# A third seven-product pair in the second feed forward, with one pair's weight sums kept in DRAM

## Chip, cores and metric

One core of one Trainium2 chip. The metric is the device time of one execution in microseconds (us): median of three runs, lower is better.

## What is computed

Two transformer blocks on x of 256 rows by 1024 columns, in fp32. The part that the change touches is the gated feed forward of the second block, and, as a place for early work, the feed forward of the first:

```python
def sq_relu_mlp(h, w1, w2):                       # first block, D_FF = 4096
    return jnp.square(jax.nn.relu(h @ w1)) @ w2

# second block, D_FF_2 = 2816
h = rmsnorm(x, norm_ffn[layer])
x = x + (jax.nn.silu(h @ w_gate[layer]) * (h @ w_up[layer])) @ w_down[layer]
return rmsnorm(x, norm_final)
```

## The kernel before

Each engine has its own program, written out by hand in the order in which it runs: `tensor_program` (TensorE, PE), `vector_program` (VectorE, DVE), `scalar_program` (ScalarE, ACT), `pool_program` (GpSimd, POOL) and `sync_program`, whose queue (SP) issues the weight loads. They meet at semaphores alone.

**Three products for one.** A weight tile of 1 MB (128 partitions x 2048) is a `Unit`. It lands in one of six slots (seven in the second feed forward), ScalarE makes its high half (`hi`, line 1185), VectorE the low half (`lo`, line 1720), two instructions of 128x1024 each. `part` (lines 511 to 513) then multiplies, for each k of the unit, high by high, high by low and low by high: four k make 12 matmuls of 128x512. I call that a product.

**The second feed forward.** The 2816 columns are eleven chunks of 256. `GROUPS` lists them as single chunks and as pairs of chunks; `PAIRS = (3,7)` makes two pairs, so that the groups are chunks 0, 1, 2, (3,4), 5, 6, (7,8), 9, 10. A single chunk takes two gate-and-up units for each of the two row blocks, 4 products, so two single chunks take 8. A pair takes 7 for the same columns, on a Winograd form of the 2x2 block product: three of the units are used as loaded, four are sums. The weight sums are made in place by VectorE (`make`, two instructions of 128x1024 for each of four sums), the input sums once (`form`). Against its 7 products a pair has 7 gate-and-up units and 2 down units to load and split, where two single chunks have 4 and 2.

**The order in a group.** `begin(g)` is the group's first product or two, `rest(g)` what follows, with the down products of group g-1 inside. After a pair, TensorE runs `begin(g + 1)` and only then turns the pair's hidden rows (`hid_turn2`, eight transposes, line 493); ScalarE and VectorE make high and low halves of the turned rows (`hid_lo2`, line 2055, semaphore `hid_lo`), and the down products of the pair, `down2(g, ...)`, wait for these. In `quad_group` VectorE makes the pair's hidden rows between splits of weight units. After the loop over groups the end is written out: the last chunk's gate-and-up product (`up2`), the down products of the last two groups, and the last turns.

**The first feed forward** (about 180 to 350 us) has `up_wide` and `down1` on TensorE; VectorE runs `sum_wide`, `low_wide`, splits, and rows of an adaptive gate (`gate_rows`). Tiles S1 and S2 (16 KB of each partition) lie idle during most of it, until `between` writes S1 again at its end.

Of the kernel before, what the change touches and what calls it, by code (L numbers as in the profile page):

```python
# [24 lines left out]
class Mem:  # L25


    def __init__(self, nc, ctx):
# [116 lines left out]
        self.FL = [M(f"FL{i}", 68 + 2 * i, [128, 4, 128], F32R) for i in range(4)]  # L145
        self.g1 = M("quad_g1", 6, [128, 512])
# [19 lines left out]
out_mm o1_hi o1_lo res1 nscale_dve nscale_act n_turned n_dve n_act kn  # L166
# [7 lines left out]
out2_mm res2 made quad_act quad gu_mm dn_mm hid2 res3 last_rows y_out y_act""".split()  # L174
# [16 lines left out]
class Unit:  # L191
# [3 lines left out]
    def __init__(self, nk, wid, pieces, split, free):  # L195
        self.nk, self.wid, self.pieces, self.split, self.free = nk, wid, pieces, split, free
        self.base = None
# [13 lines left out]
PAIRS = (3,7)  # L211
# [15 lines left out]
def weight_units(d, S):  # L227
# [68 lines left out]
    def quad_unit(g, n, src, i):  # L296
        c0 = 256 * GROUPS[g][0]
        add(("gu", g), src, 4 * i, 4, [(src, c0, 512)], True, ("gu_mm", QUAD_AT[g] + n + 1))
        return units[-1]

    loads = list(units)
    for g in range(NG + 1):
        if g < NG and GROUPS[g][1]:
            quad_unit(g, 0, "w_gate_2", 0)
            quad_unit(g, 1, "w_up_2", 0)
            at = len(units)
            down_units(g - 1)
            down = units[at:]
            quad_unit(g, 2, "w_up_2", 1)
# [4 lines left out]
            b11, t1, t2, b22, t3, b21, t4 = by["gu", g]  # L314
            loads += [b11, t1, t2, *down, t4, b22, t3, b21]
# [16 lines left out]
    for g in range(NG):  # L332
        if GROUPS[g][1]:
            q = by["gu", g]
            used += [*q[0:3], *by["dn", g - 1], *q[3:7]]
        else:
            used += by["gu", g] + (by["dn", g - 1] if g else [])
# [22 lines left out]
    for n, g in enumerate(g for g in range(NG) if GROUPS[g][1]):  # L360
# [3 lines left out]
        t1.landed, t2.landed, t4.landed, t3.landed = ((S["made"], 8 * n + 2 * i + 2) for i in range(4))  # L364
# [3 lines left out]
def sync_program(e, m, S, units, by, out, d):  # L368
# [11 lines left out]
    def load(n):  # L380
        unit = units[n]
        for old in unit.old:
            w.wait_ge(old.free[0], old.free[1])
        v = unit.block(m)
# [21 lines left out]
def pool_program(e, m, S, d):  # L406
# [20 lines left out]

    e.dma_start(m.vec[:, :], d["vec"]).then_inc(S["l_vec"], 16)
# [22 lines left out]
    w.wait_ge(S["res1"], 8)  # L451
    e.dma_start(m.g1b[:, :], d["final_g"].to_broadcast([128, D])).then_inc(S["l_gain"], 16)
    power(6)
# [5 lines left out]
    for i in range(10, 14):  # L459
        power(i)  # L460


def tensor_program(e, m, S, by):
# [331 lines left out]
    def out1(i, tb):  # L795
# [3 lines left out]
        if k0:  # L799
            frees(2 * n + tb, ("res1", 4 * tb + 2 * n + 1))  # L800
# [253 lines left out]
    def out2(j, tb):  # L1054
# [3 lines left out]
        if i:  # L1058
            frees(2 * n + tb, ("res2", 2 * tb + n + 1))
# [29 lines left out]
    def down2(g, tb, first, last, ns=(0, 1)):  # L1089
        for n in ns:  # L1090
            for i, unit in enumerate(by["dn", g]):
                part(unit, m.HH[g % 2], m.HL[g % 2], 2 * i, tb, 2 * n + tb, first and i == 0, last, "dn_mm",
# [7 lines left out]
    def begin(g):  # L1100
        if GROUPS[g][1]:
            part(by["gu", g][0], m.AH, m.AL, 0, 0, 4, True, True, "gu_mm", n_ready(2, 0))
            quad_sum(g, 1, 0, 5, True)
# [36 lines left out]
    for g in range(2, NG - 1):  # L1140
        rest(g)
        if GROUPS[g][1]:
# [8 lines left out]
    up2(NG - 1, 0)  # L1151
# [18 lines left out]
def scalar_program(e, m, S, units, by, out, d):  # L1170
# [232 lines left out]
    s = norm_squares(4, "res1", (2, 4), 0)  # L1403
# [7 lines left out]
    s = norm_squares(6, "res1", (6, 8), 1)  # L1411
# [194 lines left out]
    s = norm_squares(16, "res2", (1, 2), 0)  # L1606
# [7 lines left out]
    s = norm_squares(18, "res2", (3, 4), 1)  # L1614
# [22 lines left out]
    def quad_group(g):  # L1637
# [14 lines left out]
        hi(2)  # L1652
# [5 lines left out]
    hi()  # L1658
    silu_gate(0, 1)
# [7 lines left out]
    for i in range(4):  # L1667
        form_hi(i)
    for g in range(2, NG - 1):
# [8 lines left out]
        for tb in range(2):  # L1678
            hid_hi2(g, tb)
# [4 lines left out]
    def last_squares(tb):  # L1684
        w.wait_ge(S["kn"], 12)
        for n, (c0, cw) in enumerate(LAST[tb]):
            w.wait_ge(S["res3"], 3 * tb + n + 1)
# [15 lines left out]
def vector_program(e, m, S, units, by):  # L1703
# [354 lines left out]
    def residual1(n, tb):  # L2058
# [6 lines left out]
        tt(m.S1[:, tb, hn], bank[2 * n + tb][:, :], m.g1b[:, hn], ALU.mult, "res1")  # L2065
        w.wait_ge(S["res1"], i + 1)
        tt(m.X[:, tb, hn], m.X[:, tb, hn], m.S1[:, tb, hn], ALU.add, "res1")
# [9 lines left out]
    def norm_features(call, tb, A, B):  # L2077
# [15 lines left out]
        tt(m.AL[:, 0:4, ts], hv, m.AH[:, 0:4, ts].bitcast(F32), ALU.subtract, "kn")  # L2093
        w.wait_ge(S["n_act"], 5 * call + 5)
# [61 lines left out]

    hid_lo(0, 4, 0, 1)
    lo(2)
    hid_lo(0, 4, 1, 2)
    lo(2)  # L2160
    for tb in range(2):
        hid_lo(1, 4, tb, 3 + tb)
    lo()
    for c in range(2, 7):
# [11 lines left out]
        else:  # L2176
            gate_add()
    sum_wide(7, 0)
# [42 lines left out]

    between(0, 2)
# [438 lines left out]
```

## Time and profile before

| | |
|---|---|
| three runs | 721.14 us median (720.99 to 721.19) |
| profiled execution | 720.66 us, its span 718.9 us |
| busy share of the span | PE 99%, PE weight loads 79%, DVE 77%, ACT 59%, POOL 4% |
| DMA | 152.22 MB, mean 212 GB/s |

The span is from the first to the last record; the 1.8 us around it are the execution's start and end. A busy share says only that an engine had an instruction under way: matmuls overlap, so that each of 0.39 us starts 0.23 us after the one before. The rows that the prediction rests on stand in a section of their own.

### The profile page before, as it was taken

The numbers are of one execution on the slowest core, as the hardware profiler recorded it, in microseconds if no ns is written. First come the engines' busy times: TensorE is split into PE (matmuls) and PEld (weight loads), VectorE is DVE, ScalarE is ACT, GpSimd is POOL, SyncE is SP. The second block draws the span as 40 slices with busy tenths as digits, with TensorE's granted clock in tenths as the row PEclk, the third lists the DMA queues.
The fourth block names the chain that finished last, engine by engine and source line by source line (L and its number), as shares of the span: only waits on it lengthen the run. The fifth ranks groups of instructions, "written<-read, shape, count | busy, mean of one in ns | idle before, by whom it ended". The sixth has DMA issues, their size and how long they took to land.

```text
span 718.9 us, 9667 instructions
## 1 busy us (share of the span) xinstructions
PE 709.1 (99%) x3722; PEld 567.9 (79%) x3722; DVE 555.8 (77%) x949; ACT 424.6 (59%) x701; POOL 25.9 (4%) x43
## 2 busy tenths in 40 slices
PE   8999999999999999999999999999999999999996
PEld 4678885588888888888888777778888888888885
DVE  4789999898666757756998799855857988678933
ACT  4487658995754654546645677666456466436712
POOL 1030012001000000000010000000000000000000
PEclk9999999999999999999999999999999999999999
DMA  9996939617556585744548433344375598568501
GB/s 366 415 378 224 387 104 357 218 59 263 197 179 231 214 289 196 268 146 154 163 144 300 172 118 118 119 172 178 118 233 175 197 313 310 181 230 316 209 1 58
DMA packets 71932, 152.22 MB, mean 212 GB/s; under 512 B 4096, under 2 KB 19456, under 8 KB 70864
## 3 DMA queue, kind: packets, MB, share of 16 engines
q1 hardware_dynamic: 70080, 146.32, 57.4%
q0 software_dynamic: 1520, 5.03, 2.0%
q8 instruction: 29, 0.48, 0.3%
q10 hardware_dynamic: 288, 0.27, 0.1%
q14 instruction: 15, 0.12, 0.0%
HBM read 150.56 MB, written 1.05 MB: 211 GB/s over the span
## 4 chain that ended last, share of the span: by engine, by line
PE 91%; ACT 3%; issue 2%; DMA 2%; DVE 1%; POOL 0%; POOLq 0%; DVEq 0%; SPq 0%
PE bank L511 23%; PE bank L513 23%; PE bank L512 23%; PE bank L856 5%; PE bank L493 5%; PE bank L854 3%; DMA W<-in_w_in 2%; ACT WH L1185 1%; PE bank L530 1%; PE bank L988 1%; PE bank L1010 1%; PE bank L694 1%; PE bank L716 1%; PE bank L570 1%; PE bank L853 1%
## 5 line engine op out<-in xcount | busy, mean ns | idle before, releaser
L1720 DVE TENSOR_TENSOR WL<-W,WH 128x1024 fp32r<-128x1024 f32 (+2 forms) x234 | 263.4, 1173 | 27.0 <-ACT WH L1185 26.7
L1185 ACT ACTIVATE WH<-W 128x1024 fp32r<-128x1024 f32 (+2 forms) x234 | 222.9, 1013 | 55.7 <-DMA W<-in_w_mlp 35.8
L511 PE MATMUL bank<-WH,AHL 128*128 128x512 f32 (+1 forms) x440 | 173.1, 393 | 0.0
L513 PE MATMUL bank<-WH,AHL 128*128 128x512 f32 (+1 forms) x440 | 169.7, 386 | 0.0
L512 PE MATMUL bank<-WL,AHL 128*128 128x512 f32 (+1 forms) x440 | 169.6, 385 | 0.0
L511 PEld LDWEIGHTS bank<-WH,AHL 128*128 128x128 f32 x440 | 82.7, 188 | 19.0 <-issue 3.2
L513 PEld LDWEIGHTS bank<-WH,AHL 128*128 128x128 f32 x440 | 82.6, 188 | 16.9
L512 PEld LDWEIGHTS bank<-WL,AHL 128*128 128x128 f32 x440 | 82.8, 188 | 15.4
L511 PE MATMUL bank<-WH,HH 128*128 128x512 f32 (+1 forms) x218 | 84.9, 390 | 0.0
L513 PE MATMUL bank<-WH,HL 128*128 128x512 f32 (+1 forms) x218 | 84.5, 388 | 0.0
L512 PE MATMUL bank<-WL,HH 128*128 128x512 f32 (+1 forms) x218 | 84.4, 387 | 0.0
L856 PE MATMUL bank<-AHL,WH 128*128 128x512 f32 x168 | 60.5, 398 | 0.0
L854 PE MATMUL bank<-AHL,WL 128*128 128x256 f32 x192 | 50.0, 281 | 0.0
L513 PEld LDWEIGHTS bank<-WH,HL 128*128 128x128 f32 x218 | 40.9, 188 | 8.5
L512 PEld LDWEIGHTS bank<-WL,HH 128*128 128x128 f32 x218 | 41.0, 188 | 8.3
L511 PEld LDWEIGHTS bank<-WH,HH 128*128 128x128 f32 x218 | 40.9, 188 | 8.0
L854 PEld LDWEIGHTS bank<-AHL,WL 128*128 128x128 f32 x192 | 36.3, 189 | 2.0
L856 PEld LDWEIGHTS bank<-AHL,WH 128*128 128x128 f32 x168 | 31.6, 188 | 6.7
L1735 DVE SCALAR_TENSOR_TENSOR cacc<-hp,vec,cacc 128x256 f32<-128x256 f32 x88 | 36.0, 479 | 0.2
L413 POOL TENSOR_TENSOR stat<-stat 128x1 f32<-128x1 f32 x12 | 10.1, 846 | 594.4 <-DVE stat L1744 549.0
L1193 ACT ACTIVATE HH<-bank 128x256 fp32r<-128x256 f32 (+1 forms) x22 | 9.2, 458 | 35.7 <-PE bank L493 35.7
L2055 DVE TENSOR_TENSOR HL<-bank,HH 128x256 fp32r<-128x256 f32 (+1 forms) x22 | 10.7, 517 | 23.4 <-ACT HH L1193 23.4
(307 smaller groups left out, 937.8 us busy)
## 6 DMA issues: line engine op xcount, KB each, us to landing
W<-in_w_mlp SPq DMA_DIRECT2D x32, 1024.0 KB, 5.4
W<-in_w_in SPq DMA_DIRECT2D x24, 1024.0 KB, 5.1
W<-in_w_down SPq DMA_DIRECT2D x11, 1024.0 KB, 5.1
W<-in_w_ada SPq DMA_DIRECT2D x10, 1024.0 KB, 8.0
WX<-in_w_ada SPq DMA_DIRECT2D x10, 1024.0 KB, 10.0
W<-in_w_out SPq DMA_DIRECT2D x8, 1024.0 KB, 5.2
W<-in_w_up SPq DMA_DIRECT2D x8, 1024.0 KB, 5.1
W<-in_w_gate SPq DMA_DIRECT2D x14, 512.0 KB, 4.0
```

The source lines that it names most:

```text
L413: e.tensor_tensor(m.stat[:, 40 + i:41 + i], m.stat[:, 24 + i:25 + i], m.stat[:, 94:95], ALU.pow).then_inc(S["rstd"], 1)
L493: ins = e.transpose(bank[b][:, c * 128:c * 128 + 128], src, m.ident[:, :])
L511: e.matmul(po, hs, wh[:, k, c0:c0 + cw], start=first and k == 0, stop=False, skip_group_check=onto)
L512: e.matmul(po, hs, wl[:, k, c0:c0 + cw], start=False, stop=False, skip_group_check=onto)
L513: ins = e.matmul(po, ls, wh[:, k, c0:c0 + cw], start=False, stop=last and k == unit.nk - 1, skip_group_check=onto)
L854: ins = e.matmul(bank[4 + j][:, 0:256], wl[:, k, js], m.AH[:, 4 * i + k, :], start=False, stop=False)
L856: ins = e.matmul(both, wh[:, k, js], m.AHL[:, :, 4 * i + k, :], start=False, stop=i == 1 and k == 3)
L1185: e.activation(m.WH[unit.slot][:, c], m.W32[unit.slot][:, c], ACT.Copy).then_inc(S["w_hi"], 1)
L1193: e.activation(o, i, ACT.Copy, scale=scale).then_inc(S[sem], 1)
L1720: e.tensor_tensor(m.WL[unit.slot][:, c], m.W32[unit.slot][:, c], m.WH[unit.slot][:, c].bitcast(F32), ALU.subtract).then_inc(S["w_lo"], 1)
L1735: e.scalar_tensor_tensor(o, a, scalar, b, op0, op1).then_inc(S[sem], 1)
L2055: e.tensor_tensor(L[:, k0:k0 + nj, ts], bank[b][:, 0:nj * 128].rearrange("p (j n) -> p j n", j=nj), H[:, k0:k0 + nj, ts].bitcast(F32), ALU ...
```

## The change

- `PAIRS` becomes (2, 5, 8): groups are chunks 0, 1, (2,3), 4, (5,6), 7, (8,9), 10. There are three pairs, and the last pair now stands directly ahead of the last chunk.
- The four weight sums of the pair at chunk 2 are made in the first feed forward and kept in a DRAM tensor `sums`: POOL loads the four blocks of 128x512 that belong to one k (two loads of 512 KB), VectorE makes four sums of 128x512 in place (`kept_sums`), and POOL stores the 1 MB. There are four such steps, in two staging places (offsets 0 and 8 KB, where S1 and S2 are). The second feed forward loads these sums as units; the pairs at 5 and 8 make theirs in place as before.
- `form` and `form_hi` move ahead, since a pair now comes as the third group. After the last pair `begin` already runs the last chunk's first `up2`, so the one after the loop is left out.

```diff
-PAIRS = (3,7)
+PAIRS = (2, 5, 8)
+STORED = (2,)
+STEPS = (4, 0, 0)
+SUMS_AT = (1, 0, 1, 0, 0, 0, 2, 0, 0, 0, 0, 0, 0)
+SUMS = [[(0, 8)[s % 2] for s in range(STEPS[0])], [0] * STEPS[1], [(68, 76)[s % 2] for s in range(STEPS[2])]]
...
     def quad_unit(g, n, src, i):
...
+        if GROUPS[g][0] in STORED and n in (1, 2, 4, 6):
+            s = STORED.index(GROUPS[g][0])
+            kept = d["sums"][s, {4: 0, 2: 1, 1: 2, 6: 3}[n]].rearrange("p (k n) -> p k n", k=4)
+            units[-1].pieces = [(0, 512, kept)]
...
+    def blocks_in(phase, i):
...
+        if SUM_AT[s]:
+            w.wait_ge(landing, SUM_AT[s])
+        if i < 2 and phase == 0:
+            w.wait_ge(*((S["n_turned"], 4), (S["kn"], 4))[i])
...
+        for j, src in enumerate(("w_up_2", "w_gate_2")):
+            rows = d[src][:, c0:c0 + 512].rearrange("(h k p) n -> p k h n", h=2, p=128)[:, kt, :, :]
+            e.dma_start(place[:, 2 * j:2 * j + 2, :], rows).then_inc(landing, 16)
...
     e.dma_start(m.g1b[:, :], d["final_g"].to_broadcast([128, D])).then_inc(S["l_gain"], 16)
+    kept_sums(0)
     power(6)
...
-    up2(NG - 1, 0)
+    if not GROUPS[NG - 2][1]:
+        up2(NG - 1, 0)
     down2(NG - 2, 0, False, False, (0,))
     hid_turn2(NG - 1, 0)
     down2(NG - 2, 0, False, False, (1,))
...
+    def kept_sums(place):
+
+        for s in range(sum(SUMS_AT[:place]), sum(SUMS_AT[:place + 1])):
+            at = m.sums[sum(SUMS, [])[s]]
+            u0, u1, g0, g1 = (at[:, i, :] for i in range(4))
+            w.wait_ge(S[f"l_sums{SUM_SEM[s]}"], SUM_AT[s] + 32)
+            tt(g0, u0, g0, ALU.subtract, "made")
+            tt(u0, u1, u0, ALU.subtract, "made")
+            w.wait_ge(S["made"], 4 * s + 1)
+            tt(u1, u1, g0, ALU.subtract, "made")
+            w.wait_ge(S["made"], 4 * s + 3)
+            tt(g1, g1, u1, ALU.subtract, "made")
...
     for tb in range(2):
         hid_lo(1, 4, tb, 3 + tb)
     lo()
+    kept_sums(1)
     for c in range(2, 7):
...
             gate_add()
+        kept_sums(c)
...
+    sums_stored()
     between(0, 2)
...
-        following = GROUPS[g + 1][1]
-        make(g, 2)
+        made, following, near = in_place(g), in_place(g + 1), GROUPS[g + 1][1]
+        if made:
+            make(g, 2)
```

TensorE, after the turns of the last pair's hidden rows (HH and HL are the high and low halves of turned hidden rows, AHL the input's, WH and WL a weight unit's). Before:

```order
L511 MATMUL bank<-WH_66,AHL 128x512
L512 MATMUL bank<-WL_60,AHL 128x512
L513 MATMUL bank<-WH_66,AHL 128x512
L493 MATMUL bank<-ident,hid_164 128x128 [waits hid2]
L493 MATMUL bank<-ident,hid_164 128x128 x3
L493 MATMUL bank<-ident,hid_164 128x128 [waits quad,hid2]
L493 MATMUL bank<-ident,hid_164 128x128 x3
L511 MATMUL bank<-WH_65,AHL 128x512
L512 MATMUL bank<-WL_59,AHL 128x512
L513 MATMUL bank<-WH_65,AHL 128x512
```

and now:

```order
L572 MATMUL bank<-WH_64,AHL 128x512
L552 MATMUL bank<-ident,hid_164 128x128 [waits hid2]
L552 MATMUL bank<-ident,hid_164 128x128 x3
L552 MATMUL bank<-ident,hid_164 128x128 [waits quad,hid2]
L552 MATMUL bank<-ident,hid_164 128x128 x3
L570 MATMUL bank<-WH_66,HH_166 128x512 [waits w_lo,hid_lo]
L571 MATMUL bank<-WL_60,HH_166 128x512
L572 MATMUL bank<-WH_66,HL_168 128x512
```

Before, 24 matmuls on AHL (two products of the next chunk) follow the turns, and then the down products on HH; now a down product, which waits for `hid_lo`, follows at once. Twelve down matmuls later come the two turns of the last chunk's hidden rows, which wait for `hid2`.

VectorE, at the same place. Before (the group behind the last pair was chunk 9):

```order
L1729 TENSOR_TENSOR quad_g_224<-bank,quad_g_224 128x512 [waits gu_mm]
L1720 TENSOR_TENSOR WL_60<-W_5_54,WH_66 128x1024 [waits w_hi] x2
L1729 TENSOR_TENSOR hid_164<-g1b,rel_170 128x512 [waits quad,silu,hid_turned]
L1729 TENSOR_TENSOR hid_164<-g1b,rel_171 128x512 [waits silu]
L1720 TENSOR_TENSOR WL_57<-W_2_51,WH_63 128x1024 [waits w_hi] x2
L1720 TENSOR_TENSOR WL_55<-W_0_49,WH_61 128x1024 [waits w_hi] x2
L2055 TENSOR_TENSOR HL_168<-bank,HH_166 128x4x128 [waits hid_hi] x2
L1720 TENSOR_TENSOR WL_210<-W_6_209,WH_211 128x1024 [waits w_hi] x2
L1729 TENSOR_TENSOR hid_165<-bank,rel_170 128x256 [waits hid_turned,silu]
```

and now:

```order
L1802 TENSOR_TENSOR quad_g_228<-bank,quad_g_228 128x512 [waits gu_mm]
L1793 TENSOR_TENSOR WL_58<-W_3_52,WH_64 128x1024 [waits w_hi] x2
L1802 TENSOR_TENSOR hid_164<-g1b,rel_170 128x512 [waits quad,silu,hid_turned]
L1802 TENSOR_TENSOR hid_164<-g1b,rel_171 128x512 [waits silu]
L1793 TENSOR_TENSOR WL_60<-W_5_54,WH_66 128x1024 [waits w_hi] x2
L1793 TENSOR_TENSOR WL_57<-W_2_51,WH_63 128x1024 [waits w_hi] x2
L2128 TENSOR_TENSOR HL_168<-bank,HH_166 128x4x128 [waits hid_hi] x2
L1793 TENSOR_TENSOR WL_55<-W_0_49,WH_61 128x1024 [waits w_hi] x2
L1802 TENSOR_TENSOR hid_165<-bank,rel_170 128x256 [waits hid_turned,silu]
L2128 TENSOR_TENSOR HL_169<-bank,HH_167 128x2x128 [waits hid_hi]
```

Operation for operation the first nine rows are the same, in other slots: nothing moved on VectorE here, while TensorE's next step did.

POOL, in the first feed forward, now:

```order
L507 DMA g1b<-in_final_g 128x1024 [waits res]
L466 DMA sums_224<-in_w_up 128x2x512 [waits n_turned]
L466 DMA sums_224<-in_w_gate 128x2x512
L466 DMA sums_225<-in_w_up 128x2x512 [waits kn]
L466 DMA sums_225<-in_w_gate 128x2x512
L477 DMA sums<-sums_224 128x4x512 [waits made]
L466 DMA sums_224<-in_w_up 128x2x512 [waits l_sums0]
L466 DMA sums_224<-in_w_gate 128x2x512
L477 DMA sums<-sums_225 128x4x512 [waits made]
L466 DMA sums_225<-in_w_up 128x2x512 [waits l_sums1]
L466 DMA sums_225<-in_w_gate 128x2x512
L477 DMA sums<-sums_224 128x4x512 [waits made]
```

Between the `g1b` load and the small power instructions that follow it, POOL had nothing; it now has eight loads and four stores (the last of them is one more row like the last here).

## Rows read from the trace of the kernel before

**Rows 1.** Page, sections 1 and 2: TensorE's busy time, and its granted clock.

```profile
PE 709.1 (99%) x3722; PEld 567.9 (79%) x3722; DVE 555.8 (77%) x949; ACT 424.6 (59%) x701; POOL 25.9 (4%) x43
...
PEclk9999999999999999999999999999999999999999
```

**Rows 2.** Waits of TensorE: total us, times, longest us; first and last of three.

```profile
PE bank L570 <- POOL ones L430: 2.8, 1, 2.8
...
PE bank L610 <- POOL stat L433: 0.3, 1, 0.3
```

**Rows 3.** Timeline, TensorE, behind the last pair: start us, us, operation.

```profile
667.21 0.39 PE L511 MATMUL bank<-WH,AHL 128*128 128x512 f32 x1
...
672.65 1.03 PE L493 MATMUL bank<-ident,hid 128*128 128x128 f32 x8
673.44 0.47 PE L511 MATMUL bank<-WH,AHL 128*128 128x512 f32 x1
673.75 0.39 PE L512 MATMUL bank<-WL,AHL 128*128 128x512 f32 x1
```

**Rows 4.** Timeline, VectorE, the same stretch; in brackets idle before, and releaser.

```profile
661.97 0.69 DVE L1729 TENSOR_TENSOR g1b<-bank,g1b 128x512 f32<-128x512 f32 x1 [2.10 <-PE bank L513]
...
667.71 0.69 DVE L1729 TENSOR_TENSOR quad_g<-bank,quad_g 128x512 f32<-128x512 f32 x1
...
670.58 1.29 DVE L1729 TENSOR_TENSOR hid<-g1b,rel 128x512 f32<-128x512 f32 x2
671.78 4.63 DVE L1720 TENSOR_TENSOR WL<-W,WH 128x1024 fp32r<-128x1024 f32 x4
676.32 1.29 DVE L2055 TENSOR_TENSOR HL<-bank,HH 128x512 fp32r<-128x512 f32 x2
677.52 2.36 DVE L1720 TENSOR_TENSOR WL<-W,WH 128x1024 fp32r<-128x1024 f32 x2
679.79 0.42 DVE L1729 TENSOR_TENSOR hid<-bank,rel 128x256 f32<-128x256 f32 x1
```

**Rows 5.** Page, section 5: the weight splits, busy us, mean ns, idle before.

```profile
L1720 DVE TENSOR_TENSOR WL<-W,WH 128x1024 fp32r<-128x1024 f32 (+2 forms) x234 | 263.4, 1173 | 27.0 <-ACT WH L1185 26.7
L1185 ACT ACTIVATE WH<-W 128x1024 fp32r<-128x1024 f32 (+2 forms) x234 | 222.9, 1013 | 55.7 <-DMA W<-in_w_mlp 35.8
```

**Rows 6.** Busy time by stretch: us, engines (instructions), clock, DMA share, GB/s.

```profile
230.00:255.00 25.00, 25.00 (x130) 21.29 (x129) 15.61 (x16) 11.50 (x14) 0.00 (x0) 1.00 0.67 248
626.00:690.00 64.00, 64.00 (x291) 52.97 (x289) 51.83 (x55) 34.13 (x43) 0.00 (x0) 1.00 0.66 229
```

**Rows 7.** Timeline, VectorE, in and behind the first feed forward.

```profile
207.46 1.29 DVE L2055 TENSOR_TENSOR HL<-bank,HH 128x512 fp32r<-128x512 f32 x2 [5.08 <-ACT HH L1193]
...
234.71 2.36 DVE L1720 TENSOR_TENSOR WL<-W,WH 128x1024 fp32r<-128x1024 f32 x2 [5.41 <-ACT WH L1185]
...
326.09 0.69 DVE L2127 TENSOR_REDUCE hid<-bank 128x256 f32<-128x512 f32 x1 [8.08 <-PE bank L856]
...
338.51 0.69 DVE L1729 TENSOR_TENSOR S<-bank,g2b 128x512 f32<-128x512 f32 x1 [1.50 <-PE bank L513]
```

**Rows 8.** DMA issues: a weight load, and POOL's slowest large one, us to landing.

```profile
W<-in_w_mlp SPq DMA_DIRECT2D x32, 1024.0 KB, 5.4
...
g2b<-in_b_ada POOLq DMA_DIRECT2D x1, 512.0 KB, 8.3
```

**Rows 9.** Busy time by stretch, behind the last matmul (columns as in rows 6).

```profile
713.00:714.00 1.00, 0.00 (x0) 0.00 (x0) 0.93 (x4) 0.86 (x4) 0.00 (x0) 1.00 0.00 0
...
717.00:718.00 1.00, 0.00 (x0) 0.00 (x0) 0.00 (x0) 0.00 (x0) 0.00 (x0) 0.80 0.91 338
```

**Rows 10.** Timeline, TensorE, the first microseconds.

```profile
2.76 5.25 PE L570 MATMUL bank<-ones 128*128 128x512 f32 x6 [2.76 <-POOL ones L430]
...
11.51 1.02 PE L570 MATMUL bank<-ones 128*128 128x512 f32 x2
```

**Rows 11.** Timeline, POOL: the instruction that TensorE waited for there.

```profile
2.48 0.22 POOL L430 MEMSET ones<- 128x128 f32 x1
```

More of the change, by code:

```diff
@@ L303, in weight_units @@
         if g < NG and GROUPS[g][1]:
+            kept = GROUPS[g][0] in STORED
+            first = len(units)
             quad_unit(g, 0, "w_gate_2", 0)
             quad_unit(g, 1, "w_up_2", 0)
[L306 to L309, printed above, removed]
+            if not kept:
+                at = len(units)
+                down_units(g - 1)
+                down = units[at:]
+                quad_unit(g, 2, "w_up_2", 1)
+            else:
+                down_units(g - 1)
+                quad_unit(g, 2, "w_up_2", 1)
             quad_unit(g, 3, "w_up_2", 1)
@@ L313, in weight_units @@
             quad_unit(g, 6, "w_gate_2", 1)
-            b11, t1, t2, b22, t3, b21, t4 = by["gu", g]
-            loads += [b11, t1, t2, *down, t4, b22, t3, b21]
+            if kept:
+                loads += units[first:]
+            else:
+                b11, t1, t2, b22, t3, b21, t4 = by["gu", g]
+                loads += [b11, t1, t2, *down, t4, b22, t3, b21]
             continue
@@ L359, in weight_units @@
         unit.lo = (S["w_lo"], 2 * u)
-    for n, g in enumerate(g for g in range(NG) if GROUPS[g][1]):
+    for n, g in enumerate(g for g in range(NG) if GROUPS[g][1] and GROUPS[g][0] not in STORED):
         t1, t2, _, t3, _, t4 = by["gu", g][1:]
@@ L363, in weight_units @@
             unit.base = unit.landed
-        t1.landed, t2.landed, t4.landed, t3.landed = ((S["made"], 8 * n + 2 * i + 2) for i in range(4))
+        t1.landed, t2.landed, t4.landed, t3.landed = ((S["made"], 4 * len(SUM_SEM) + 8 * n + 2 * i + 2) for i in range(4))
     return units, loads, by
@@ L458, in pool_program @@
     e.dma_start(m.g2b[:, :], d["norm_final"].to_broadcast([128, D])).then_inc(S["l_gain"], 16)
-    for i in range(10, 14):
-        power(i)
+    kept_sums(1)
+    power(10)
+    power(11)
+    power(12)
+    power(13)
 def tensor_program(e, m, S, by):
@@ L1651, in quad_group @@
         e.activation(m.rel[1][:, :], m.g1[:, :], ACT.Silu).then_inc(S["silu"], 1)
-        hi(2)
+        if not GROUPS[g + 1][1]:
+            hi(2)
+        for tb in range(2):
+            hid_hi2(g, tb)
+        if GROUPS[g + 1][1]:
+            hi(2)
     silu_gate(0, 0)
@@ L1658, in scalar_program @@
     hi()
+    if GROUPS[2][1]:
+        for i in range(4):
+            form_hi(i)
     silu_gate(0, 1)
@@ L1666, in scalar_program @@
         hid_hi2(1, tb)
-    for i in range(4):
-        form_hi(i)
+    if not GROUPS[2][1]:
+        for i in range(4):
+            form_hi(i)
     for g in range(2, NG - 1):
@@ L2496, in vector_program @@
     gated(1, 0, 0)
-    lo()
+    sums_stored()
+    if GROUPS[2][1]:
+        form(0)
+        form(1)
+        lo()
+        form(2)
+        form(3)
+    else:
+        lo()
     gated(0, 1)
@@ L2502, in vector_program @@
     hid_lo2(0, 1)
-    lo()
-    for i in range(4):
-        form(i)
+    if GROUPS[2][1]:
+        for i in range(4):
+            form_lo(i)
+        lo()
+    else:
+        lo()
+        for i in range(4):
+            form(i)
     for tb in range(2):
         hid_lo2(1, tb)
-    for i in range(4):
-        form_lo(i)
+    if not GROUPS[2][1]:
+        for i in range(4):
+            form_lo(i)
     for g in range(2, NG - 1):
```

143 lines of the change are left out of this document (102 added, 41 removed).

## The prediction

> **What bounds the kernel now.** I read the page first, then TensorE's waits, then the timelines of TensorE and VectorE at the place where the order changes.
>
> TensorE is busy for 709.1 of 718.9 us at a granted clock of full level throughout [rows 1]. Its list of waits has three rows that sum to 3.4 us, all in the first 12 us of the kernel [rows 2]. So behind the start TensorE never waits for data: the kernel is as long as TensorE's list of instructions. A change pays only if it shortens that list, and only as long as every other engine stays ahead.
>
> The price of a matmul is not the 0.39 us of its row but the distance between starts. From 667.21 to 672.65 us, where `begin` runs two products, there are 24 matmuls of 128x512 [rows 3], 5.44 us or 0.227 us each. A product of 12 is therefore 2.72 us.
>
> **The change, step by step.**
>
> *TensorE's work.* Three pairs take the place of two, so two more chunks are computed as a pair: 7 products instead of 8. One product leaves the list: **-2.72 us**. Down products and transposes (4 for a chunk) are the same in number. The middle groups' transposes are done in five visits instead of six, and a visit makes the first matmul behind it slower, 0.31 instead of 0.23 us (673.44 to 673.75) [rows 3]; that is 0.1 us at most, and I take nothing for it.
>
> *The end of the second feed forward.* The last pair now stands directly ahead of the last chunk. On TensorE the eight turns of the pair's hidden rows were followed by 24 matmuls of the next chunk's second half, 5.44 us in which the halves of the turned rows were made. Now the first down product of the pair follows them at once, and waits for `hid_lo`. VectorE's own list at that place is the same, instruction for instruction, so that the time at which it gets there can be read from before. There it starts a sum at 661.97 as soon as TensorE releases it (idle 2.10 us before, so nothing is carried over from earlier), and from there on it has no gap: sums, splits, the two hidden rows at 670.58, four halves of splits at 671.78, and the low halves of the turned rows at 676.32 [rows 4]. The first of these two takes 0.69 us (the length of one such instruction alone, as at 667.71) and ends at 677.01. TensorE has done its turns at 673.44 [rows 3]. The wait is 677.01 - 673.44 = 3.57 us, and 0.06 us from the end of a releaser to the start of the matmul, which I take from the start of the kernel (a memset that ends at 2.70, a matmul that starts at 2.76) [rows 10, 11]: **+3.63 us**. Bounds: below, 0 if VectorE got there by TensorE's pace; above, 3.63 and another split of 2.27 us if one slipped in ahead, 5.9. The row is for the same list, so I take 3.63.
>
> *Behind it.* Twelve down matmuls run, 2.72 us and 0.08 for the slower first one, from 677.07 to 679.87. Then come the turns of the last chunk's hidden rows. VectorE must first finish its second low half, two halves of a split and the hidden row, which in the rows ends at 679.79 + 0.42 = 680.21 [rows 4]; with 0.06 this is 680.27: **+0.40 us**. What is queued behind on TensorE is the rest of the down products and the last chunk, all of it on the path to the end, so both waits count in full.
>
> *Splits.* Three more weight units have to be loaded and split (9 for a pair, 6 for two single chunks). Six more halves cost VectorE 1.13 us each, since four take 4.54 us from start to next start [rows 4], 6.8 us, and ScalarE at most 6 x 1.01 = 6.1 us [rows 5]. The cover is VectorE's idle time in that stretch; in the last 64 us of it VectorE was busy 51.8 us and ScalarE 34.1 [rows 6]. I cost them at nothing, and come back to the cover among the rivals.
>
> *Weight sums in place.* Two pairs make theirs in place before, two do now: nothing. The stored sums replace loads of weights by loads of the same size.
>
> *Sums in the first feed forward.* Sixteen instructions of 128x512 at up to 0.69 us [rows 7], about 10 us in all: 2.5 after the second chunk's splits, 2.5 after chunk 2, 5 after the gate's sum. VectorE is busy 15.6 of 25 us there [rows 6], and each of the three places stands ahead of an idle time: 5.08, 5.41 and 8.08 us [rows 7]. All hidden, with 2.6, 2.9 and 3.1 us to spare.
>
> *Transfers.* POOL issues eight loads of 512 KB and four stores of 1 MB, 8 MB more in the first feed forward; the slowest load of 512 KB on its queue landed in 8.3 us [rows 8]. The stores are last needed when `between` writes S1 at 338.51 [rows 7]. VectorE's idle time ahead of 326.09 begins at 318.0, and eight sums at 0.61 us from start to start bring it to 322.9, where the last store is issued. That leaves 15.6 us for 2 MB: a weight load of 1 MB takes 5.4 us, so two in a row 10.8; by the slow row four times 512 KB would be 33 [rows 8]. Rows for 1 MB are nearer, so the stores are hidden. Weight loads share the bandwidth, at 0.67 of the engines' time [rows 6], and some will land later; what stands ahead of them are VectorE's idle times of 5 and 8 us. On POOL's queue the small power instructions stand behind the stores, and are wanted only behind 338.51 as well. I take nothing; bounds are 0 and some 3 us.
>
> *Sum.* -2.72 + 3.63 + 0.40 = **+1.31 us**. The profiled execution of 720.66 us would become 721.97; the median of the runs was 721.14, 0.5 above the profiled one, which gives **722.4 us**. The sum is 0.18% of the kernel's time, and about 0.2% (1.44 us) is what a measurement can tell from no change, so this very forecast lies at the border of the two verdicts.
>
> **The rivals.**
>
> *The clock falls in the new wait (slower).* The wait is the first in this kernel behind the start that stops TensorE for several microseconds: 3.6, or 4.4 if the eight transposes ahead of it are not counted as work. In the profile the granted clock is still 1.00 from 713 to 717 though TensorE's last matmul is over by 713, and is 0.80 in the microsecond from 717 to 718, so that it fell from 2.4 to 1.2 GHz about 4.6 us after the last matmul [rows 9]. That speaks against a fall within 3.6 us, and not strongly. The price: the first six matmuls of the kernel take 5.25 us, 0.87 each, where two of the same form take 1.02, 0.51 each, at 11.51 [rows 10] (the clock column reads full for both, the durations do not). Half speed for the 5 us of the first six costs half of it, 2.6 us. It decides if the clock has fallen when the first down product starts; then the time is 722.4 + 2.6 = 725.0. The Trainium skill, "TensorE: Matmul & The Clock Gate", section "HAM oscillation — how this bites in real kernels", says that a wait for data in the middle of a kernel puts the array back to half clock, so that the matmuls behind it run slow. By that rule the time is that of this rival, by the row it is 722.4.
>
> *The wait is not there (faster).* If the low halves came in time, only the product is left: 721.14 - 2.72 = 718.4. For it: splits are a little early when loads land early. Against it: VectorE's chain begins with a release by TensorE itself and has no gap [rows 4], so no earlier load can shorten it. It would take VectorE 3.6 us faster over a stretch of 15.
>
> *VectorE becomes the bound (slower).* The period from pair to pair was a pair and two single chunks, 64 us of TensorE's time (626 to 690), of which VectorE was busy for 51.8 [rows 6]. Now one single chunk leaves it: 72 matmuls and 4 transposes, 16.8 us, on TensorE, but only six halves (6.8 us) and four small instructions, about 8.2 us, on VectorE. That makes VectorE busy 43.6 of 47.2 us. The 3.6 us left must hold the 2.1 us that VectorE waits for TensorE in each pair [rows 4]; 1.5 are spare. If its waits for ScalarE and for loads take more than that, TensorE waits 1 to 2 us in each of the last two pairs: 722.4 + 3 = 725.4.
>
> *The early transfers get in the way (slower).* If the last stores land later than 338.51, `between` waits, and with it TensorE: up to 3 us, 725.4.
>
> **How the numbers follow.** The forecast's mechanism has 0.70, with an error of some 0.5 us either way; within it 722.58 (1.44 above) is passed a little less often than not. The clock has 0.12, VectorE 0.06, the transfers 0.05, the missing wait 0.07. Within 0.2%: 0.43, out of the 0.70 and nothing else. Slower: 0.27 of the 0.70, and 0.23 of the three slower rivals, 0.50. Faster: 0.07. The range goes from 721.6 (the forecast with both waits at their shorter end) to 725.2, which holds the clock's case and most of the other two; left out are the missing wait and a tail above, not 2 in 10.
>
> **What would show it.** Right: TensorE's waits list two new rows near the end, about 3.6 us for VectorE's HL (line 2128) and 0.4 for a hidden row; 12 fewer matmuls; VectorE's sums in the first feed forward with no new wait of TensorE there; the last pair's turns about 2.7 us earlier behind the same start of the feed forward. Wrong: no wait behind the last pair's turns; matmuls of 0.45 us from start to start or a clock below 1.00 behind it; TensorE waiting for low halves of weights inside the pairs; VectorE waiting for a store at the end of the first feed forward.

## The result

The median of five runs is **723.73 us** (723.52 to 725.47), beside 721.00 us for the kernel before on the same occasion: a ratio of 1.0041, 95% interval 1.0027 to 1.0056. The change makes the kernel 2.7 us slower. The forecast was 722.4 us in a range of 721.6 to 725.2, with "slower" the likeliest outcome at 0.50. The range holds the time, but the forecast's own case does not give it: 1.3 us are missing from its sum.

### Profile after

The page, first its section on busy time, then the row of TensorE's granted clock (the answers to [rows 1]):

```profile
span 721.5 us, 9683 instructions
...
PE 707.8 (98%) x3710; PEld 566.5 (79%) x3710; DVE 574.9 (80%) x972; ACT 430.8 (60%) x704; POOL 34.6 (5%) x55
...
PEclk9999999999999999999999999999999999999999
```

TensorE has 12 instructions fewer, and yet the span is 2.6 us longer. The clock row shows nothing: in slices of 18 us a short fall is rounded away. The waits of TensorE (against [rows 2]; total us, times, longest us), the first of five:

```profile
PE bank L570 <- DVE HL L2128: 3.4, 1, 3.4
```

It is the new one; the other four are within the first 57 us. The timeline of TensorE behind the last pair (start us, us, operation) shows it, and shows something behind it as well:

```profile
686.96 1.03 PE L552 MATMUL bank<-ident,hid 128*128 128x128 f32 x8
691.38 0.50 PE L570 MATMUL bank<-WH,HH 128*128 128x512 f32 x1 [3.38 <-DVE HL L2128]
691.72 0.40 PE L571 MATMUL bank<-WL,HH 128*128 128x512 f32 x1
...
692.43 0.46 PE L571 MATMUL bank<-WL,HH 128*128 128x512 f32 x1
692.68 0.63 PE L572 MATMUL bank<-WH,HL 128*128 128x512 f32 x1
693.11 0.63 PE L570 MATMUL bank<-WH,HH 128*128 128x512 f32 x1
...
695.24 0.63 PE L572 MATMUL bank<-WH,HL 128*128 128x512 f32 x1
695.67 0.56 PE L552 MATMUL bank<-ident,hid 128*128 128x128 f32 x2
...
696.31 0.39 PE L571 MATMUL bank<-WL,HH 128*128 128x512 f32 x1
```

The eight turns take 0.79 us of TensorE's time (in [rows 3] the next matmul starts 0.79 us after them), so that TensorE is free at 687.75 and starts at 691.38: a wait of 3.63 us, of which the row names 3.38, since it counts idle time from the modelled end of the last transpose. The first matmuls behind the wait start 0.34 us and then some 0.24 us apart. Then seven of them are 0.43 us apart, and from 696.31 on it is 0.23 again. The busy time by stretch (us; busy us of PE, weight loads, DVE, ACT, POOL; then clock, DMA share, GB/s) names the cause:

```profile
692.00:693.00 1.00, 1.00 (x5) 0.84 (x4) 1.00 (x2) 0.00 (x0) 0.00 (x0) 0.81 0.00 0
693.00:694.00 1.00, 1.00 (x4) 0.71 (x4) 1.00 (x2) 0.00 (x0) 0.00 (x0) 0.50 0.00 0
...
695.00:696.00 1.00, 1.00 (x6) 0.70 (x4) 0.00 (x0) 0.00 (x0) 0.00 (x0) 0.50 0.00 0
696.00:697.00 1.00, 1.00 (x7) 0.83 (x6) 0.25 (x1) 0.39 (x1) 0.00 (x0) 0.98 0.00 0
```

0.50 is the lower level, 1.2 GHz. A mean of 0.81 over a microsecond means that 0.38 us of it were at that level, so the clock fell at 692.62; by the same reckoning on the last row it was back at 696.04. That is 3.4 us at half speed, and it began 4.9 us after the last turn and 1.2 us *after* the work had started again.

VectorE at the same place (against [rows 4]):

```profile
676.28 0.69 DVE L1802 TENSOR_TENSOR g1b<-bank,g1b 128x512 f32<-128x512 f32 x1 [2.10 <-PE bank L572]
...
690.64 1.28 DVE L2128 TENSOR_TENSOR HL<-bank,HH 128x512 fp32r<-128x512 f32 x2
...
694.10 0.42 DVE L1802 TENSOR_TENSOR hid<-bank,rel 128x256 f32<-128x256 f32 x1
```

It is the list of before, 14.3 us later, with the same idle time of 2.10 us ahead. And the early sums in the first feed forward (against [rows 7]):

```profile
202.78 2.62 DVE L1802 TENSOR_TENSOR sums<-sums 128x512 f32<-128x512 f32 x4
207.67 1.29 DVE L2128 TENSOR_TENSOR HL<-bank,HH 128x512 fp32r<-128x512 f32 x2 [2.27 <-ACT HH L1257]
...
217.30 2.36 DVE L1793 TENSOR_TENSOR WL<-W,WH 128x1024 fp32r<-128x1024 f32 x2 [2.75 <-ACT WH L1249]
...
232.22 2.62 DVE L1802 TENSOR_TENSOR sums<-sums 128x512 f32<-128x512 f32 x4
234.80 2.36 DVE L1793 TENSOR_TENSOR WL<-W,WH 128x1024 fp32r<-128x1024 f32 x2
...
318.17 5.15 DVE L1802 TENSOR_TENSOR sums<-sums 128x512 f32<-128x512 f32 x8
...
326.30 0.69 DVE L2201 TENSOR_REDUCE hid<-bank 128x256 f32<-128x512 f32 x1 [2.98 <-PE bank L915]
...
338.89 0.69 DVE L1802 TENSOR_TENSOR S<-bank,g2b 128x512 f32<-128x512 f32 x1 [1.67 <-PE bank L572]
```

The first and the last sums leave idle time over. Those in the middle leave none: the split behind them starts as they end, at 234.80, in place of 234.71 before. The reason is ahead of them: the split at 217.30 stood at 214.29 before, because its weight unit landed 3 us later, and what follows it came 3 us later too, up to the middle sums. POOL's first store had been issued at 205.69; that it held the unit up is likely but not shown. The write to S1 at 338.89 waits for TensorE's bank as before, not for a store.

### One measure for all kernels

Executions differ by several tenths before the second feed forward begins, in the landing of the first weight loads above all. So I also compare, within each profiled execution, the distance from the last turns ahead of the second feed forward to the last matmul of the kernel. Before:

```profile
540.54 1.04 PE L493 MATMUL bank<-ident,S 128*128 128x128 f32 x8
...
712.61 0.28 PE L513 MATMUL bank<-WH,HL 128*128 128x256 f32 x1
```

and now:

```profile
540.77 1.04 PE L552 MATMUL bank<-ident,S 128*128 128x128 f32 x8
...
715.35 0.28 PE L572 MATMUL bank<-WH,HL 128*128 128x256 f32 x1
```

172.07 us have become 174.58, 2.51 more. I call this distance the second part; for the variants it is read from the same two rows.

### The profile page after: what moved, and what is told of

Read it like the earlier page. It is cut to its first block, busy times and chain, and to the rows that moved or that the text cites. A ratio compares the mean times of both kernels' runs of the same rounds, so it can differ in the third digit from the quotient of the medians.

```text
span 721.5 us, 9683 instructions
## 1 busy us (share of the span) xinstructions
PE 707.8 (98%) x3710; PEld 566.5 (79%) x3710; DVE 574.9 (80%) x972; ACT 430.8 (60%) x704; POOL 34.6 (5%) x55
## 4 chain that ended last, share of the span: by engine, by line
PE 88%; DMA 3%; ACT 3%; DVE 3%; issue 2%; SPq 0%; POOLq 0%; POOL 0%; DVEq 0%
PE bank L570 22%; PE bank L572 22%; PE bank L571 22%; PE bank L915 5%; PE bank L552 5%; PE bank L913 3%; DVE WL L1793 2%; DMA W<-in_w_in 2%; DMA WX<-in_w_ada 1%; ACT WH L1249 1%; PE bank L589 1%; PE bank L1047 1%; PE bank L1069 1%; PE bank L753 1%; PE bank L775 1%
## 5 line engine op out<-in xcount | busy, mean ns | idle before, releaser
L1793 DVE TENSOR_TENSOR WL<-W,WH 128x1024 fp32r<-128x1024 f32 (+2 forms) x240 | 270.5, 1174 | 24.3 <-ACT WH L1249 24.0
L1249 ACT ACTIVATE WH<-W 128x1024 fp32r<-128x1024 f32 (+2 forms) x240 | 228.8, 1013 | 64.8 <-DMA W<-in_w_mlp 36.3
L570 PE MATMUL bank<-WH,AHL 128*128 128x512 f32 (+1 forms) x420 | 165.3, 393 | 0.0
L572 PE MATMUL bank<-WH,AHL 128*128 128x512 f32 (+1 forms) x420 | 162.0, 386 | 0.0
L571 PE MATMUL bank<-WL,AHL 128*128 128x512 f32 (+1 forms) x420 | 161.8, 385 | 0.0
L570 PEld LDWEIGHTS bank<-WH,AHL 128*128 128x128 f32 x420 | 79.0, 188 | 18.5 <-issue 3.2
L572 PEld LDWEIGHTS bank<-WH,AHL 128*128 128x128 f32 x420 | 78.9, 188 | 16.3
L571 PEld LDWEIGHTS bank<-WL,AHL 128*128 128x128 f32 x420 | 79.0, 188 | 14.7
L1257 ACT ACTIVATE HH<-bank 128x512 fp32r<-128x512 f32 (+1 forms) x20 | 9.0, 487 | 31.0 <-PE bank L552 31.0
L2128 DVE TENSOR_TENSOR HL<-bank,HH 128x512 fp32r<-128x512 f32 (+1 forms) x20 | 10.5, 554 | 11.0 <-ACT HH L1257 11.0
```

The costliest lines, as they stand in the source:

```text
L570: e.matmul(po, hs, wh[:, k, c0:c0 + cw], start=first and k == 0, stop=False, skip_group_check=onto)
L571: e.matmul(po, hs, wl[:, k, c0:c0 + cw], start=False, stop=False, skip_group_check=onto)
L572: ins = e.matmul(po, ls, wh[:, k, c0:c0 + cw], start=False, stop=last and k == unit.nk - 1, skip_group_check=onto)
L1249: e.activation(m.WH[unit.slot][:, c], m.W32[unit.slot][:, c], ACT.Copy).then_inc(S["w_hi"], 1)
L1257: e.activation(o, i, ACT.Copy, scale=scale).then_inc(S[sem], 1)
L1793: e.tensor_tensor(m.WL[unit.slot][:, c], m.W32[unit.slot][:, c], m.WH[unit.slot][:, c].bitcast(F32), ALU.subtract).then_inc(S["w_lo"], 1)
```

## The experiments

Theory A: the change costs the wait at the end and a fall of the clock in it, and nothing else. Its rival, theory B: the 1.4 us beyond the forecast's sum come from the early part (sums, transfers, stores) or the start. All variants start from the changed kernel. The results together; the last column is the second part against the 172.07 us of before:

| variant | median us | ratio to before (95%) | second part |
|---|---|---|---|
| the changed kernel | 723.73 | 1.0041 (1.0027 to 1.0056) | +2.51 |
| wait filled | 723.27 | 1.0026 (1.0016 to 1.0036) | +1.30 |
| wait covered | 718.50 | 0.9964 (0.9951 to 0.9976) | -2.74 |
| two pairs | 721.89 | 1.0006 (0.9997 to 1.0015) | +0.06 |
| halves first | 720.71 | 0.9993 (0.9984 to 1.0001) | -0.88 |
| the changed kernel again | 724.25 | 1.0040 (1.0028 to 1.0053) | +2.48 |
| longer wait | 726.24 | 1.0068 (1.0055 to 1.0082) | +4.55 |
| wait of 2.7 us | 723.71 | 1.0034 (1.0024 to 1.0044) | +1.30 |
| adjacent pairs | 729.04 | 1.0109 (1.0094 to 1.0125) | +7.12 |
| half covered | 719.99 | 0.9984 (0.9975 to 0.9993) | -1.39 |
| half covered, halves first | 718.68 | 0.9966 (0.9952 to 0.9979) | -2.74 |

The medians of before beside the variants were 721.23 to 721.28, beside the first row 721.00.

### The wait filled with work that nobody reads

```diff
+    take(5)
+    for i in range(15):
+        unit = by["gu", NG - 1][1]
+        e.matmul(bank[5][:, :], m.AH[:, 4 + i % 4, 0:128], m.WH[unit.slot][:, i % 4 * 512:i % 4 * 512 + 512],
+                 start=True, stop=True)
     down2(NG - 2, 0, False, False, (0,))
```

> The changed kernel with 15 matmuls of 128x512 whose result nobody reads, into the free bank 5, between the last pair's turns and its first down product. The work and VectorE's dates stay as they are, only TensorE isn't idle: 15 x 0.227 = 3.4 us of the 3.63 are filled. Theory A (the wait costs 3.63 + 0.40 us, and the rest of the loss is the clock that falls in it): the granted clock is 1.00 throughout, TensorE waits about 0.2 us for HL and 0.4 to 0.5 for the hidden row, and the time is the forecast's sum on the median of before, 721.0 + 1.31 = 722.3, 1.4 under the changed kernel. Theory B (the 1.4 us come from elsewhere: the sums and transfers of the first feed forward, or the start): the time stays at 723.7.

TensorE's timeline and one stretch of its busy time:

```profile
687.27 1.03 PE L552 MATMUL bank<-ident,hid 128*128 128x128 f32 x8
688.07 3.69 PE L1217 MATMUL bank<-WH,AHL 128*128 128x512 f32 x15
691.69 0.50 PE L570 MATMUL bank<-WH,HH 128*128 128x512 f32 x1
```

```profile
692.00:694.00 2.00, 2.00 (x10) 1.64 (x9) 2.00 (x3) 0.00 (x0) 0.00 (x0) 1.00 0.00 0
```

The first down product starts 4.42 us after the turns, as in the changed kernel (686.96 to 691.38): nothing was moved. But the clock stays at 1.00, and the second part is +1.30 us, the forecast's +1.31 within a hundredth. The clock's fall costs 2.51 - 1.30 = **1.2 us**. By the median the variant missed what was expected, 723.27 in place of 722.3. The spans say what part of that is outside: their median is 720.9 against 719.4 for before, +1.5, and three of the eight runs took 2.5 to 3.0 us around the span, where the others took 1.9 to 2.1 and the runs of before 1.8. So some 0.2 us lie in the start of the span and the rest around it.

### The wait covered

```diff
         up2(NG - 1, 0)
+    up2(NG - 1, 1)
     down2(NG - 2, 0, False, False, (0,))
...
     down2(NG - 1, 0, False, True)
-    up2(NG - 1, 1)
     down2(NG - 2, 1, False, False, (0,))
```

> The changed kernel with the last chunk's second gate-and-up product (24 matmuls, 5.44 us) moved up to stand directly behind the last pair's turns. Theory A: the wait of 3.63 us is covered, so are the 0.40 behind it, the clock doesn't fall, and of the change only the product is left: 721.0 - 2.72 = 718.3, no wait of TensorE behind the start; if its new place close to the end costs a wait there, up to 0.5 us more. Theory B (1.4 us lost elsewhere): 719.7.

All of TensorE's waits, and the clock where it fell before:

```profile
PE bank L629 <- POOL ones L485: 2.8, 1, 2.8
PE bank L610 <- DMA WX<-in_w_ada: 0.8, 1, 0.8
PE bank L610 <- DMA W<-in_w_ada: 0.7, 1, 0.7
PE bank L552 <- ACT hTc L1278: 0.6, 1, 0.6
```

```profile
692.00:694.00 2.00, 2.00 (x11) 1.65 (x10) 2.00 (x3) 0.00 (x0) 0.00 (x0) 1.00 0.00 0
```

Both waits and the fall are gone; the four rows are all within the first 58 us. The second part is 2.74 us shorter than before, the product's 2.72, and the median 718.50 is 2.7 under its 721.23. The move of two lines turns the change from 0.4% slower into 0.36% faster. Between the filled and the covered variant lie 4.04 us, the two waits that the forecast put at 3.63 + 0.40. There is no room for theory B in the second part.

### The early part alone

```diff
-PAIRS = (2, 5, 8)
+PAIRS = (2, 7)
```

> The changed kernel with PAIRS = (2, 7): the early sums, the DRAM tensor and the transfers of the first feed forward stay, but there are two pairs as before and the last one has two single chunks behind it. Theory A: nothing is gained and nothing lost, 721.0 within 0.3. Theory B (the early part costs the 1.4 us): 722.4.

The second part is that of before within 0.06 us. The median is 0.66 above the one of before, and the interval of the ratio holds 1; theory A wanted nothing here and theory B 1.4, so that the median alone decides for neither. The traces do. The eight turns that stand ahead of the first feed forward, and the next eight turns on S, behind it; before, and then in this variant:

```profile
179.84 1.03 PE L493 MATMUL bank<-ident,S 128*128 128x128 f32 x8
...
349.19 1.03 PE L493 MATMUL bank<-ident,S 128*128 128x128 f32 x8
```

```profile
180.97 1.03 PE L552 MATMUL bank<-ident,S 128*128 128x128 f32 x8
...
350.32 1.03 PE L552 MATMUL bank<-ident,S 128*128 128x128 f32 x8
```

They are 169.35 us apart in both, and 169.34 or 169.35 us apart in the traces of the changed kernel and of every variant. So the sums, loads and stores of the first feed forward cost TensorE nothing, and of theory B only the start is left. The profile of this run is 1.44 us late at the last turns ahead of the second part (541.98 against 540.54), but of that 1.08 had come by 98.8 us (against 97.75), long before POOL's first load of the new kind at 181 us, and the rest comes behind 385 us. The profiled execution of before was itself an early one: its span of 718.9 is below all of the 24 spans taken beside this variant (719.0 to 720.3). What is left over is about 0.4 us: in all kernels of the table but the one with a wait of 2.7 us, the median lies 0.0 to 0.7 us above what the second part gives. From 0.1 to 0.3 us of it lie around the span (1.9 to 2.1 us in these eleven runs, 1.8 to 1.9 in those of before). Where the rest comes from is not shown; it isn't the first feed forward.

### The order of halves and splits

```diff
+        if g == NG - 2:
+            hi()
+            hid_hi2(g, 0)
+            hi()
+            hid_hi2(g, 1)
+            return
...
+        elif g == NG - 2:
+            lo()
+            hid_lo2(g, 0)
+            lo()
...
-    lo()
     gated(NG - 1, 0)
+    hid_lo2(NG - 2, 1)
+    lo()
     hid_lo2(NG - 1, 0)
```

> The changed kernel with the halves of the last pair's turned rows made ahead of the splits (ScalarE and VectorE: one split, the first row block's halves, one split, the last chunk's hidden row, the second row block's halves, one split). The first low halves are then ready one split of 2.3 us earlier. Theory A: a wait of about 1.35 us, 0.2 to 0.3 more inside the first down product for its second unit's split, none for the hidden row, and no fall of the clock in so short a wait: 721.0 - 2.72 + 1.6 = 719.9, 3.8 under the changed kernel. If the clock falls in 1.4 us too: 721.5. Theory B: 721.3, with the clock at 1.00.

VectorE, then TensorE:

```profile
688.75 0.69 DVE L2134 TENSOR_TENSOR HL<-bank,HH 128x512 fp32r<-128x512 f32 x1
```

```profile
687.35 1.03 PE L552 MATMUL bank<-ident,hid 128*128 128x128 f32 x8
689.49 0.50 PE L570 MATMUL bank<-WH,HH 128*128 128x512 f32 x1 [1.11 <-DVE HL L2134]
```

The low half ends at 689.44 and the down product starts 0.05 us later, with a wait of 689.49 - 688.14 = 1.35, as expected. The clock is 1.00 throughout, and the second part -0.88: -2.74 and 1.86 of waits, 0.25 more than expected, inside the first down product. All eleven runs agree within 1.0 us. A wait of 1.35 us left the clock alone.

### Once more, and a longer wait

The changed kernel again, to have it on the chip of the variants:

> The changed kernel once more, unchanged, beside the runs of before on the same chip, so that it can be compared with the variants. The trace of the filled variant gives 27.19 us from the last pair's turns to the last matmul, the first trace of the changed kernel 28.39. Theory A (the clock falls each time, 1.2 us): 723.7 within 0.3, a clock near 0.996. Theory C (the fall is a matter of chance from run to run): runs in two groups, near 722.5 and 723.7.

The second part is +2.48, and again the clock fell, at 693.5, and was back at 696.9, 3.4 us in all. In the ten runs of this kernel the mean clock was 0.994 to 0.997, in those of before 0.997 to 0.999. Three of the ten, at 0.994, had spans 1 to 2 us longer than most of the others; no profile shows those. Then the longer wait:

```diff
-            hi(2)
+            hi(3 if g == NG - 2 else 2)
...
-            lo(2)
+            lo(3 if g == NG - 2 else 2)
             for tb in range(2):
                 hid_lo2(g, tb)
```

(The split of the loop's end is left out in turn, on both engines.)

> The changed kernel with one more split ahead of the last pair's low halves on ScalarE and VectorE: the wait grows by 2.27 us to 5.9 and the 0.40 behind it goes. Theory A1 (after a stop the clock falls some 5 us behind the last work, 692.6 - 687.7 us in the first trace, however the wait ends): it is low when the first down product starts, about 1 us earlier than its matmuls in the order of work, and the half level costs 1.7 to 2.2 us in place of 1.6: 723.7 + 1.9 + 0.0 to 0.6 = 725.6 to 726.2. Theory A2 (the chip gives the clock back only after a fixed time of work, so that the price doesn't grow with the wait): 725.6.

TensorE's first matmul behind the wait, and the stretches:

```profile
694.62 0.80 PE L570 MATMUL bank<-WH,HH 128*128 128x512 f32 x1 [5.65 <-DVE HL L2127]
```

```profile
693.00:694.00 1.00, 0.00 (x0) 0.00 (x0) 1.00 (x2) 0.00 (x0) 0.00 (x0) 1.00 0.00 0
694.00:695.00 1.00, 0.38 (x1) 0.38 (x2) 1.00 (x2) 0.00 (x0) 0.00 (x0) 0.60 0.00 0
...
697.00:698.00 1.00, 1.00 (x5) 0.82 (x4) 0.00 (x0) 0.00 (x0) 0.00 (x0) 0.69 0.00 0
```

The wait is 5.9 us. The clock fell at 694.20, 5.5 us after the turns and just before the work, and was back at 697.62: again 3.4 us. The second part is +4.55: -2.74, 5.89 of wait, and 1.40 of clock. The price of the clock hardly grew with the wait, since the half level lasted as long as before, and its first 0.4 us now fell into the wait itself. The median of 726.24 is at the upper end of what was expected.

### A shorter wait at the same end

Four of the unread matmuls in place of fifteen.

> The changed kernel with 4 matmuls that nobody reads behind the turns: 0.9 us of the wait are filled, 2.7 are left. The end of the wait stays where it is. Theory A1 (a fall about 5 us behind the last work, in whatever state TensorE is then): the clock still falls, later by 0.9 us, and the time stays at 723.7. Theory A3 (a wait has to be about as long as 3.6 us to bring the clock down): it stays at 1.00 and the time is that of the filled variant, 1.2 under the changed kernel.

```profile
687.93 1.17 PE L1217 MATMUL bank<-WH,AHL 128*128 128x512 f32 x4
691.55 0.50 PE L570 MATMUL bank<-WH,HH 128*128 128x512 f32 x1 [2.45 <-DVE HL L2131]
```

```profile
692.00:694.00 2.00, 2.00 (x11) 1.61 (x10) 2.00 (x3) 0.00 (x0) 0.00 (x0) 1.00 0.00 0
```

Neither theory alone holds. In the profiled run the clock did not fall, and the second part is the filled variant's +1.30. But of the eight runs two have spans of 720.6 at a mean clock of 0.998, and six have 721.5 to 722.8 at 0.995 or 0.996. No profile shows one of the six; by span and mean clock they are runs with the fall. So with 2.7 us of wait the fall seems a matter of the run, six times in eight, and the median, 723.71, is one of those six.

### Three pairs off the end

```diff
-PAIRS = (2, 5, 8)
+PAIRS = (2, 5, 7)
```

> The changed kernel with PAIRS = (2, 5, 7): three pairs still, two single chunks behind the last one as before the change, but the last two pairs stand side by side. If the place at the end were the only cost: 721.0 - 2.72 = 718.3 and no wait. The rival that VectorE becomes the bound: a pair costs TensorE 108 matmuls less overlap, VectorE nine units to split and four sums; without a single chunk in between (16.8 us of TensorE's time against 8.2 of VectorE's, 8.6 us of slack) the second of the two pairs must wait for low halves of weights, some 6 to 9 us in rows of TensorE waiting for WL: 718.3 + 6 to 9 = 724.3 to 727.3, more if the clock falls in them.

TensorE's wait in all, its longest piece, and the clock around it:

```profile
PE bank L570 <- DVE WL L1793: 8.0, 5, 3.0
```

```profile
644.58 0.60 PE L552 MATMUL bank<-ident,hid 128*128 128x128 f32 x4
648.22 0.47 PE L570 MATMUL bank<-WH,HH 128*128 128x512 f32 x1 [3.04 <-DVE WL L1793]
```

```profile
640.00:660.00 20.00, 14.18 (x59) 10.53 (x60) 17.08 (x18) 9.27 (x12) 0.00 (x0) 1.00 0.34 107
```

Here VectorE is the bound, in the second of the two neighbouring pairs. The second part is +7.12, 9.9 us above the covered variant: the 8.0 of the row, and 1.9 us that the row doesn't count, since it starts each wait at the modelled end of the matmul before and the matmuls behind a wait are a little slower. The size was put too low (6 to 9). The longest wait is 3.2 us (four turns, 0.4 us, from 644.58; the next matmul at 648.22), and a wait of 2.5 us ends 6.5 us before it does. Yet the clock stays at 1.00 in this trace. Two of the four runs had spans 1 us longer still, at a mean clock of 0.994; no profile shows those. So the pairs have to be spaced, and with three of them in eleven chunks the last one ends up at the end.

### Half measures, and both together

Half of the product moved:

```diff
-    down2(NG - 2, 0, False, False, (0,))
-    hid_turn2(NG - 1, 0)
-    down2(NG - 2, 0, False, False, (1,))
-    down2(NG - 1, 0, False, True)
-    up2(NG - 1, 1)
+
+    def downs():
+        down2(NG - 2, 0, False, False, (0,))
+        hid_turn2(NG - 1, 0)
+        down2(NG - 2, 0, False, False, (1,))
+        down2(NG - 1, 0, False, True)
+
+    up2(NG - 1, 1, None, downs)
```

> The changed kernel with only the first half of the last chunk's second gate-and-up product (12 matmuls, 2.72 us) moved up behind the last pair's turns; the second half stays at its place. If the price is the uncovered rest of the wait: 3.63 - 2.72 = 0.91 us for HL and 0.4 to 0.5 for the hidden row, no fall of the clock, 721.2 - 2.72 + 0.91 + 0.45 = 719.9. If a new wait at the last chunk's second row block comes (the work between its two places is 12 matmuls shorter): up to 1 us more.

The second part is -1.39, that is -2.74 and 1.35 of waits, as expected (0.91 + 0.45); 719.99 us, and no fall. Then this with the halves first:

> Both repairs in their smaller form: 12 matmuls moved up as in the half-covered variant, and the low halves ahead of the splits as in the variant with the halves first. 2.72 us of cover against the 1.6 us of wait that were left there: no wait, no fall of the clock, 718.5 like the fully covered variant, within 0.3. If the halves' new place on ScalarE or VectorE costs something by itself, it is over 718.8.

The second part is -2.74, the same to the hundredth as in the covered variant, and 718.68 us. Two ways lead to the same end; the covered variant is the simpler.

## Why the prediction was right, and where it was wrong

The two waits and the saved product were right within a hundredth or two of a microsecond, and give 722.4. That the range held 723.73 is owed to its upper end, which had been drawn to take in the case of the clock, a rival with 0.12: the time lies about as far above the forecast's 722.4 as under that rival's 725.0. So the range was right in part by luck. The sign of being wrong that came was the one of the clock: matmuls 0.43 us from start to start and a clock below 1.00 behind the wait.

**The product, -2.72.** Right: -2.74 where nothing else is in the way. The missing visit of transposes, taken for nothing, is worth nothing.

**The wait for the low halves, +3.63.** Right to the hundredth, 687.75 to 691.38. The step that carried it was that VectorE's list at that place is unchanged and starts from a release by TensorE, so that its dates could be taken from the rows of before. The whole list came 14.3 us later, unchanged.

**The wait for the hidden row, +0.40.** Right as a quantity: the filled variant minus the covered one is 4.04. In the changed kernel it isn't seen, because the slowed matmuls reach the turns only at 695.67, when the row, done at 694.52, has long been there.

**Work counted as hidden.** The early sums took 10.2 us (forecast 10), and left 2.27 and 2.98 us of idle time at the first and last place (forecast 2.6 and 3.1), but nothing at the middle one, where the forecast had 2.9 to spare: the splits ahead of it came 3 us later than before. It was enough, but only just, and the forecast had not seen it. The last store was issued at 323.61 (322.9), and no one waited for it. VectorE's load from pair to pair:

```profile
640.00:687.00 47.00, 47.00 (x213) 38.87 (x211) 42.66 (x45) 26.93 (x33) 0.00 (x0) 1.00 0.63 224
```

42.7 us busy in 47.0, forecast 43.6 in 47.2, and TensorE busy in all of them.

**The clock: the step that failed.** The rival was there, with 0.12. Two sentences put it that low. One was that the clock had stayed full for about 4.6 us after the last matmul of the kernel [rows 9], which "speaks against a fall within 3.6 us". The other was that the rival "decides if the clock has fallen when the first down product starts". The row was right, and the second sentence wrong: here the clock was lowered late, and though work had begun again meanwhile. In the changed kernel it was still full when the wait ended, and fell 1.2 us later, 4.9 us after the turns. The 4.6 us of the row were not a protection for waits shorter than that, but much the same delay: the falls in the three traces came 4.9 to 5.5 us after the last work. The price was too high in its turn, 2.6 us from the start of the kernel, where it measured 1.2: 3.4 us at half speed are 1.7 of lost work, less the 0.4 that would have been a wait anyhow, and 0.1 that I can't place. The Trainium skill, "TensorE: Matmul & The Clock Gate", section "HAM oscillation — how this bites in real kernels", says that the matmuls behind a wait for data start at half clock. The trace of the longer wait agrees from the first matmul on (0.59 us to the next start, then 0.43). That of the changed kernel agrees only in that matmuls behind the wait are slowed: the first five ran at full level, and the measurement decides.

**The sum.** 1.31 + 1.20 = 2.51 of the 2.73 us between the medians; 0.2 are the start and what lies around the span.

**The other rivals.** The wait was there. VectorE did not become the bound, and does so as soon as a single chunk between pairs is taken out. The early transfers stopped nothing that TensorE waited for: its first feed forward is as long as before, to 0.01 us.

**Two readings.** The third of TensorE's waits of before is not in the first 12 us but ends at 15.2, which changes nothing. And one sign was wrong as a sign: the last pair's turns did not come 2.7 us earlier behind the start of the second feed forward but 14.1 us later (146.19 against 132.11 us), because the pair stands one chunk further on, 16.8 us of work, less the 2.7 of the product.

## What to carry over

When a step is moved on the engine that bounds the kernel, ask what stood behind it: here the change saved a product of 2.7 us and with the same table took away the 5.4 us of other work that had stood behind the turns and hidden the halves of the turned rows. If the waiting engine's releaser has an unchanged list, its dates can be read from the trace of before, and here the new wait followed to a hundredth. And a wait of TensorE can cost more than its length: in these runs one of 3.6 or 5.9 us cost another 1.2 or 1.4 us for the clock, one of 2.7 us about as much in most runs, and one of 3.2 us in the traced run of another order nothing. Give it a price even where the clock is still full when the wait ends, and look for it in stretches of a microsecond, since the page's slices don't show it.

## What the runs showed of the hardware

- The clock fell 4.9, 5.1 and 5.5 us after TensorE's last work in the three traces with a fall: in the two of the changed kernel 1.2 and 1.5 us after the next matmul had started, in the one of the longer wait 0.4 before it.
- A wait of 1.35 us didn't bring it down in the trace, nor, by a mean clock of 0.998 or 0.999, in the ten other runs. One of 2.7 us did in six runs of eight, as far as mean clock and span tell; the one traced run is without a fall. Waits of 3.6 and 5.9 us did in the three profiles shown and, as far as mean clock and span tell, in all fourteen runs. With adjacent pairs a wait of 3.2 us passed at a clock of 1.00 in the one trace. So the length alone doesn't tell whether the clock falls; what else enters is open.
- Each time the half level lasted 3.4 us, whatever the wait's length. A matmul of 128x512 then starts 0.43 us after the one before, in place of 0.23.
- The mean clock of a run tells little: 0.997 is found in profiles with a fall and without one. Only the stretches show it.
